# Mixture-of-experts layers of a decoder step: the last expert pair is combined by a matmul, the last weight loads are reordered, the slots are permuted

## The reference

```python
def hier_moe(x, router, router_bias, w_gate, w_up, w_down):
    aff = jax.nn.sigmoid((xt @ router).astype(jnp.float32))
    # best of 4 groups of 8 experts, then the best two experts in it
    wts = jnp.take_along_axis(aff, eidx, axis=1)
    wts = wts / jnp.sum(wts, axis=-1, keepdims=True)
    gate = jnp.einsum('nk,nke->ne', wts, jax.nn.one_hot(eidx, N_EXPERTS))
    for g in range(MOE_GROUPS):
        hg = jax.nn.silu(einsum('nd,edf->nef', xt, w_gate[sl])) * einsum('nd,edf->nef', xt, w_up[sl])
        hg = hg * gate[:, sl, None]
        out = out + jnp.einsum('nef,efd->nd', hg, w_down[sl])
x = layer_norm(DEEPNORM_ALPHA * x + hier_moe(x, ...), ln_ffn_g, ln_ffn_b)
```

## Time and profile before

| | |
|---|---|
| three runs | 1261.54, 1262.03, 1263.52 us; median 1262.03 us |
| profiled execution | 1261.95 us, span 1260.2 us |
| PE busy | 1086.8 us, 86% of the span |
| DVE, ACT, POOL busy | 441.6, 224.2, 144.0 us |
| DMA | 309.33 MB; 423 to 424 GB/s while an expert layer streams its weights |
| expert layer 0, loop | from about 465 us to 706 us |
| expert layer 1, loop | from about 997 us to 1235 us |

### The profile page before, as it was taken

How to read it: one execution, slowest core, us unless ns; L and a number is a source line. 1 busy time by engine, 2 the same in 40 slices (tenths; PEclk the granted TensorE clock), 3 DMA queues, 4 the chain that set the end, 5 groups by cost and what they waited for, 6 DMA issues and landing times. The chain is left out here.

```text
span 1260.2 us, 13846 instructions
## 1 busy us (share of the span) xinstructions
PE 1086.8 (86%) x4872; PEld 564.5 (45%) x4872; DVE 441.6 (35%) x1143; ACT 224.2 (18%) x521; POOL 144.0 (11%) x212
## 2 busy tenths in 40 slices
PE   6999995758999879999889398899898999988880
PEld 4777774547434443333323245455544533333330
DVE  0027775565654543212111432222103531221115
ACT  0101112211200311212111213322103121211112
POOL 0000001251000010111110023130000011111000
PEclk9999997885999979999989798999999899999995
DMA  5333346000054799999998577255308699999964
GB/s 221 132 133 133 131 163 250 1 34 6 1 218 199 291 364 381 425 423 423 423 424 343 177 261 222 70 168 199 127 8 323 240 392 423 423 422 424 423 263 135
DMA packets 51726, 309.33 MB, mean 245 GB/s; under 512 B 12818, under 2 KB 13714, under 8 KB 30290
## 3 DMA queue, kind: packets, MB, share of 16 engines
q1 hardware_dynamic: 39666, 293.32, 58.1%
q0 software_dynamic: 11264, 12.61, 3.0%
q10 hardware_dynamic: 736, 2.62, 0.7%
HBM read 300.61 MB, written 30.97 MB: 263 GB/s over the span
## 5 line engine op out<-in xcount | busy, mean ns | idle before, releaser
L1202 PE MATMUL ps<-ring,xsT 128*64 128x512 f32 x704 | 165.1, 623 | 30.5 <-DMA ring<-in_experts 26.0
L302 PE MATMUL ps<-XT,ring 128*128 128x320 f32 x640 | 174.0, 435 | 11.3 <-DMA ring<-in_w_in 11.3
L302 PEld LDWEIGHTS ps<-XT,ring 128*128 128x128 f32 x640 | 122.5, 192 | 62.4 <-issue 12.3
L1202 PEld LDWEIGHTS ps<-ring,xsT 128*64 128x64 f32 x704 | 56.0, 144 | 137.0 <-issue 130.3
L1524 DVE TENSOR_TENSOR work<-work,ps 128x256 f32<-128x256 f32 x32 | 13.4, 420 | 272.6 <-ACT work L1282 272.6
L1229 PE MATMUL ps<-ring,hT 128*64 128x512 f32 x352 | 80.4, 598 | 2.2 <-DVE hT L1529 1.7
L1334 POOL DMA_INDIRECT y_dram<-ys,index x32 | 32.1, 1004 | 378.4 <-DVE ys L1535 378.4
L1202 PE MATMUL ps<-hi,xsT 128*64 128x512 f32 x320 | 70.9, 595 | 4.6 <-DMA hi<-in_experts 4.5
L1326 POOL DMA_INDIRECT XT<-x_dram,index x32 | 32.7, 1023 | 334.7 <-DVE index L1470 153.1
L1128 PE MATMUL ps<-C 128*128 128x512 f32 x124 | 70.0, 682 | 0.0
L1282 ACT ACTIVATE work<-ps 128x256 f32<-128x256 f32 x32 | 12.3, 384 | 279.8 <-PE ps L1202 279.8
(11 more groups left out here) (307 smaller groups left out, 1361.0 us busy)
## 6 DMA issues: line engine op xcount, KB each, us to landing
ring<-in_experts SPq DMA_DIRECT2D x40, 2048.0 KB, 27.3
ring<-in_experts SPq DMA_DIRECT2D x52, 1024.0 KB, 25.0
hi<-in_experts SPq DMA_DIRECT2D x20, 2048.0 KB, 27.1
ring<-in_w_in SPq DMA_DIRECT2D x10, 2048.0 KB, 7.9
hi<-in_experts SPq DMA_DIRECT2D x20, 1024.0 KB, 32.3
ring<-in_latent SPq DMA_DIRECT2D x60, 256.0 KB, 4.5
ring<-in_w_out SPq DMA_DIRECT2D x4, 2048.0 KB, 12.8
ring<-in_state SPq DMA_DIRECT2D x4, 1024.0 KB, 8.6
```

The source lines that it names most:

```text
L302: mm = pe.matmul(ps[:, q, 0:TOK], ring[:, u, k * 512 + q * P:k * 512 + (q + 1) * P], XT[:, k, :], start=(k == 0), stop=(k == KD - 1))
L1202: mm = pe.matmul(ps[e * SLOTS:(e + 1) * SLOTS, GU[p], :].rearrange("p (g f) -> p g f", g=2), xsT[:, p, k, e * SLOTS:(e + 1) * SLOTS], w[:, ...
```

## The change

**Down weights ahead of the last gate-up, in halves.** SP issues the gate-up of pairs up to 14 as before, then the down weights of pairs 14 and 15, and then the gate-up of pair 15 as four half loads: the first four of the eight slices of both experts, then the last four, which count on a semaphore of their own (`late_in`). `gate_up(15)` waits for the second halves in its middle. On PE it stands behind `down(14)`; on ACT and DVE its silu and its product stand behind the copies of pair 14.

**Last pair combined from PSUM.** DVE makes, at the start of the loop, a matrix of 128 slots by 320 tokens with the router's weight where a token of pair 15 sits (`weigh`), PE turns it, ACT copies it to `comb`. Behind the last copies PE multiplies `comb` with `ys` of pair 15: two 512-column matmuls for each of the three token tiles (`combine`). Weights of rows that came through `y_dram` are `wk_far`, which is zero where the row belongs to pair 15. Pair 15 is still scattered, since further windows may need it.

**Other rows loaded beside it.** When the scatters of pairs 0 to 14 have landed (`scattered`), SP issues all six reads of `y_dram`. They go to `places`, which is the ring slot of the second expert of pair 14. DVE adds three of the six tiles ahead of its copy of the last pair and three behind it. `y_dram` is set to zero once, in the SSD mixer, by five stores of 512 KB.

**Permuted slots.** The row of numbers that is compared with a token's place (`iota1`) is permuted: the token of rank r sits in slot 4r for r below 16, and in slot 4(r-16)+1 for r from 16 to 31.

```diff
-    c[:, CONST["iota1"]] = np.arange(1, P + 1)
+    c[:, CONST["iota1"]] = i // 64 * 64 + i % 4 * 16 + i % 64 // 4 + 1
...
+                    sp.wait_ge(zeros_set, 1)
+                    for i in range(2 * TOK // P):
+                        sp.dma_start(y_dram[i * P:(i + 1) * P, :], lnp[:, 0, :]).then_inc(y_cleared, 16)
...
-                        stream(sp, 4, PAIRS + 1)
+                        for j in range(4, LAST):
+                            gate_up_pair(j)
+                            down_pair(j - 1)
+                        down_pair(LAST - 1)
+                        down_pair(LAST)
+                        sp.wait_ge(gu_done, LAST - 2)
+                        for half, landed in enumerate((None, late_in)):
+                            for i in pair(LAST):
+                                load_half_gate_up(sp, layer, i, slot(i), half, landed)
+                        sp.wait_ge(scattered, 1)
+                        for t in range(NT):
+                            for k in range(2):
+                                r, row = ROWS[t], k * TOK + OFF[t]
+                                sp.dma_start(places[k * NT + t][0:r, :], y_dram[row:row + r, :]).then_inc(got_in[k * NT + t], 16)
...
+                    def combine():
+                        for t in range(NT):
+                            for n in range(2):
+                                mm = pe.matmul(ps[0:ROWS[t], 2 * t + n, :], comb[:, OFF[t]:OFF[t] + ROWS[t]],
+                                               ys[:, LAST % 2, n * 512:(n + 1) * 512], start=True, stop=True)
+                            mm.then_inc(comb_done, 1)
...
+                            if j == LAST and k == KD // 2:
+                                pe.wait_ge(late_in, 32)
...
                         for j in range(PAIRS):
-                            if j + 1 < PAIRS:
+                            if j + 1 < LAST:
                                 idle_work(1, MAP)
                                 gate_up(j + 1)
                             turn_hidden(j)
                             if j + 2 < PAIRS:
                                 turn(w, j + 2)
                             down(j)
+                            if j + 1 == LAST:
+                                gate_up(LAST)
...
+                            if j == LAST:
+                                pool.wait_ge(ys_out[0], PER_WINDOW * w + 16 * (PAIRS // 2))
+                                pool.wait_ge(ys_out[1], PER_WINDOW * w + 16 * (PAIRS // 2 - 1))
+                                pool.sem_inc(scattered, 1)
+                                for got in got_in:
+                                    pool.wait_ge(got, 16)
                             scatter(j)
...
+                    def weigh(each):
+                        last = pair_of[:, :, :, LAST]
+                        each.mark(v.tensor_tensor(wk_here[:, :, :], last, wk[:, :, :], ALU.mult))
+                        each.mark(v.tensor_tensor(wk_far[:, :, :], wk_here[:, :, :], inw[:, :, :], ALU.mult))
+                        for t in range(NT):
+                            ins = v.tensor_scalar(onehot[:, 0, t, :], onehot[:, 0, t, :], wk_here[:, 0, t:t + 1], None, ALU.mult)
+                        each.mark(v.tensor_tensor(wk_far[:, :, :], wk[:, :, :], wk_far[:, :, :], ALU.subtract))
+                        for t in range(NT):
+                            ins = v.scalar_tensor_tensor(out=onehot[:, 1, t, :], in0=onehot[:, 1, t, :],
+                                                         scalar=wk_here[:, 1, t:t + 1], in1=onehot[:, 0, t, :],
+                                                         op0=ALU.mult, op1=ALU.add)
+                        ins.then_inc(weighed, 1)
...
-                        v.wait_ge(y_dve, PAIRS)
+                        v.wait_ge(x_scaled, 1)
+                        gathered(each, 0, 0)
+                        gathered(each, 0, 1)
+                        gathered(each, 1, 0)
+                        rows_out(w, LAST)
+                        gathered(each, 1, 1)
+                        summed_up(w, 0)
+                        gathered(each, 2, 0)
+                        gathered(each, 2, 1)
+                        each.settle(v)
                         v.sem_inc(arrived, 1)
+                        summed_up(w, 1)
+                        summed_up(w, 2)
                         meet(v, w)
```

More of the change, by code:

```diff
@@ L55 @@
 MAX_WINDOWS = TOK // SLOTS
-PHASE_SEMS = 48
+PHASE_SEMS = 54
+LAST = PAIRS - 1
 NEG = -1e30
@@ L212, in load_gate_up, with load_half_gate_up @@
                          a["experts"][layer * EXPERTS + i][:, 0:2 * KD * FF]).then_inc(gate_up_in[i % RING], 16)
-        def load_half_gate_up(sp, layer, i, slot, half):
+        def load_half_gate_up(sp, layer, i, slot, half, landed=None):
             def part(x):
@@ L219, in load_half_gate_up @@
             sp.dma_start(part(slot[:, 0:2 * KD * FF]),
-                         part(a["experts"][layer * EXPERTS + i][:, 0:2 * KD * FF])).then_inc(gate_up_in[i % RING], 16)
+                         part(a["experts"][layer * EXPERTS + i][:, 0:2 * KD * FF])
+                         ).then_inc(gate_up_in[i % RING] if landed is None else landed, 16)
         def load_down(sp, layer, i, slot):
@@ L1304, in _ @@
                         act.sem_inc(arrived, 1)
+                        act.activation(spare[:, 1:2], eps[:, 0:1], ACT.Sqrt)
                         meet(act, w)
[L1307 to L1310 removed]
                     if layer == 0:
                         columns_in(act, 1)
[L1313 removed]
+                    statistics(act, 1, NT * act.snap(n_windows, min_val=1, max_val=MAX_WINDOWS))
                     if layer == 0:
@@ L1541, in _ @@
                         indices(each)
-                        count_windows(each)
+                        once = Tally(dve)
+                        with v.If(w < 1):
+                            once.loop(step.base + step.n)
+                            count_windows(once)
+                            combine_weights(once)
+                            once.settle(v)
+                        weigh(each)
                         rows_in(0)
                         with v.If(w < 1):
-                            once = Tally(dve)
-                            once.loop(step.base + step.n)
-                            combine_weights(once)
                             residual(once)
```

145 lines of the change are left out of this document (89 added, 56 removed).

## The result

| | before | after |
|---|---|---|
| median | 1261.78 us (1261.52 to 1263.52, 4 runs) | 1244.95 us (1243.58 to 1245.55, 4 runs) |
| profiled execution, span | 1261.95, 1260.2 | 1245.52, 1243.8 |
| ratio | | 0.9865, 95% interval 0.9849 to 0.988 |

With five rounds on another chip the same kernel came to 0.986 (0.9838 to 0.9882). The forecast was 1245, faster.

What follows compares the result with a forecast made beforehand. Expert layers were taken as bound by their weight stream, whose DMA engines end unevenly, with serial work behind it. Terms of -8.3 us (layer 1) and -8.7 (layer 0) gave -17.0 from 1261.95: 1245, range 1240 to 1250.

Steps and rivals of the forecast that it cites:

- What follows T: From T, the end of DVE's last copy: -7.9 us to layer 1's last norm, -7.7 in layer 0.
- T against L: From L, the last weights' landing, to T, the end of DVE's last copy: 10.0 us, not 7.4; +2.6 per layer.
- The clock's term: PE's slower clock behind the idle gap ahead of the last gate-up: +0.6 us in each layer (0 to 2).
- The start: Added DVE work delays the first turn of token rows and so the weight stream: +0.9 us per layer (0.2 to 2.0).
- the zeroing at 0: Zeroing `y_dram` by five stores in the SSD mixer, ahead of loads used far later, costs 0.
- Small packets: Half loads in the weight stream move at 392 GB/s against 423: +0.5 us per layer (0 to 0.8).
- The slots: Permuted slots even out the DMA engines at the stream's end: -5.0 us in layer 1, -5.6 in layer 0.
- The sum: All terms together: -8.3 us in layer 1 and -8.7 in layer 0, -17.0 in all, to 1245.
- the slots even nothing out: Rival: the stream's tail stays as uneven as before, landings gain nothing from permutation; 1255.6 us, chance 0.14.
- Late reads: Rival: other rows land late, DVE's copy of pair 15 waits 1 to 3 us; with slow clock 1250, chance 0.16.
- The late gate-up: Rival: last gate-up, issued about 1196, lands 38 us later, +14 us in each layer; 1273, chance 0.06.

Runs made afterwards that it cites:

- The filled kernel: Changed kernel with router filler, later turn of the router's weights, quartered last gate-up half, and work without use ahead of gate-up 15: 1239.46 us, 0.9821 of before.
- the router's filler: Changed kernel with four more matmuls without use ahead of the router's first matmuls: 1244.7 us, 0.9827 of the kernel before.
- the bunched slots: Kernel before with another slot permutation that puts the first ranks of every expert on the same few DMA engines: 1295.66 us, 1.0243 of before.
- quarters: Changed kernel with the last half of pair 15's gate-up load cut in two again: 0.987 of the kernel before.
- the reverse-filled kernel: Changed kernel with the slots of odd pairs filled in reverse order: 1245.06 us, 0.985 of the kernel before.
- the zeroing alone: Kernel before with only the zeroing of y_dram added (memset, five stores and their waits): 1266.61 us, 0.9998 of before.
- perm_only: Kernel before with the permuted slots and nothing else: 1254.69 us, 0.9927 of before.
- old_order: Changed kernel with whole gate-up 15 back in its old place and DVE's copy of pair 15 ahead of all additions: 1254.95 us, 0.9912 of before.

## Why the prediction was right, point by point

**What follows T.** Forecast -7.9 and -7.7 in layers 1 and 0, measured -7.8 and -7.2. The reads that the first three additions needed had landed, three additions stood ahead of the copy, and behind the first two combining matmuls DVE waited for none. In layer 0 PE waited 2.29 us for the attention's weights, which I had left out; that more than covers the missing 0.5.

**T against L.** 10.0 and 0.6 of clock forecast; 9.9 in layer 0 and 10.7 in layer 1 measured. The clock's term came out as nothing in layer 0 behind a gap of 2.27 us and 0.7 in layer 1 behind 4.18. I had said that the first half has slack for a slow clock. In layer 1 it took 6.1 us for the 5.5 between the landings, and that is where the loss comes from. The filled kernel, with 8.2 in both layers, shows what this clock hid.

**The start.** +0.9 forecast in each layer. Layer 1: +0.7. Layer 0: this step failed, in its reason and, from indices to turn, in its sign. I read the wait between the indices and the first turn in layer 1 and took it for both. In layer 0 of the kernel before, the gather waited for the store of `x_dram` and went out 1.7 us behind the indices. Now the indices came 3.2 later and the store 1.5 later, so the gather went out 1.9 later, and the first turn came 2.1 later, 1.1 closer to the indices. The stream of layer 0 therefore started 2.1 late where I had 0.9. The 3.2 were in no term of mine: 1.5 stand ahead of the store already, where the clock falls at 414 us in every kernel with the zeroing, and 1.7 come in the router's matmuls (7.6 before, 9.3 now), of which the router's filler took the slow clock away. I put the zeroing at 0, on the ground that nothing in SP's queue behind it is needed soon; that looked at the queue and not at PE's clock. Whether the zeroing makes that shift is not shown beyond the mark in the window.

**Small packets.** +0.5 forecast. Without the permutation the stream is 0.1 and 0.7 longer than before, which holds the new order of the loads as well.

**The slots.** Forecast -5.0 and -5.6; in the new kernel, -5.9 in layer 1 and -5.3 in layer 0, in the old one -5.2 and -6.1. The mechanism is shown by the bunched slots. By the Trainium skill, "DMA: Bandwidth & Descriptors", section on the descriptor swizzle, an estimate with 20 rows for every expert would have been -4.6 and -5.2. The page tells its map for one transfer to 128 partitions; the runs here agree with it for gathers and scatters by index, in direction and roughly in size: 13.2 and 14.6 us of stream for the bunched slots where 18 were worked out from it.

**The sum.** Layer 1 came to -8.9 against -8.3. Layer 0 came to -11.1 from its indices on and -7.9 with the 3.2 ahead of them, against -8.7. That the total fell on the forecast within 0.6 us, by the spans, owes something to luck: the start of layer 0 was 1.2 worse and its tail 0.5 worse than forecast, T - L of layer 0 and the stream of layer 1 were each 0.7 better, and these errors have nothing to do with each other.

**The rivals.** That the slots even nothing out is refuted. The changed kernel without the permuted slots is what it would have been, and by its ratio of 0.9951 it comes to the 1255.6 that I gave the rival. Late reads did not come true: they were issued 12 us ahead of T in layer 1 and 10 in layer 0, where the last of the six landed 1.1 behind T, and DVE waited for none of them. The room was small, since the third addition ended 0.39 ahead of the copy in layer 1 and 0.12 in layer 0; a microsecond more would have been paid there. The late gate-up did not come true either: its loads landed 22 to 25 us after their issue, so backlog had made the 39.6.

## What to carry to other kernels

A stream over many DMA engines ends with its slowest engine: when the share falls long before the last landing, look for small transfers that touch few partitions, and spread them. What decides behind the last landing is only the work that can't be done ahead of it. Cut that, but look at the gap ahead of it: quarters behind gaps of 3.9 and 4.1 us ran at half the clock and gained nothing, and with the gap filled T - L fell by 2 us. And ask of each step in each layer what comes last there: indices 2.5 us earlier were worth nothing where the gather waited for a store.

## What the runs showed of the hardware

A gap of 1.61 us in PE's work, the same in both kernels, was followed by 3.65 us for 16 records at a granted clock of 1.00 in the kernel before, and by 5.35 us at a clock that fell to 0.50 for some 3 us in the changed one.

The length of a gap alone did not tell the clock behind it. Ahead of the last gate-up, gaps of 1.93 and 2.26 us (filled), 2.27 (the changed kernel, layer 0) and 2.29 and 2.31 (before) were followed by the full clock. Gaps of 2.10 and 2.29 were followed by half of it, in the reverse-filled kernel and in the zeroing alone, both in layer 0:

```profile
685.25 5.29 PE L1245 MATMUL ps<-ring,xsT 128*64 128x512 f32 x16 [2.10 <-DMA ring<-in_experts]
```

```profile
688.01 8.78 PE L1207 MATMUL ps<-ring,xsT 128*64 128x512 f32 x32 [2.29 <-DMA ring<-in_experts]
```

The same goes for gaps of 2.02 and 2.17 in `perm_only` and `old_order`. All twelve gaps of 3.84 to 9.15 us ahead of a last gate-up were followed by half the clock.

Uneven rows in the gathers and scatters lengthened the stream of weights beside them by 5 to 6 us in some 225, though the queue that carries them moved only 12.61 of 311.96 MB in the changed kernel.
